# Dense attention stage: values become the stationary operand of the weighting, transposed probabilities stream in two float32r parts, and VectorE takes tile work up once per unit

## What is computed

```
q = axial(rms_norm(q, qn_b));  k = axial(rms_norm(k, kn_b))      # two rotations of 32 dims
s = einsum('bqhgd,bkhd->bhgqk', q, k) * 64 ** -0.5               # prompt: 512 keys, sample: 1024 keys
p = softmax(s, axis=-1)
o = einsum('bhgqk,bkhd->bqhgd', p, v)
```

## Time and profile before

| | |
|---|---|
| median of 3 runs | 3947.97 us (3947.69 to 3953.81) |
| profiled execution | 3949.25 us, span 3947.4 us |
| dense stage | 0 to about 673 us of the span |
| busy over the span | PE 96%, PEld 90%, DVE 67%, ACT 53%, POOL 22% |
| granted TensorE clock, mean | 0.986 |

### The profile page before, as it was taken

One profiled execution on the slowest core, in us unless ns is written; L12 is line 12 of the kernel. 1 busy time (PEld: TensorE's weight loads), 2 busy tenths in 40 slices (PEclk: granted clock), 3 DMA queues, 4 the chain that ended last, 5 costly groups with the idle time before them and its releaser, 6 DMA issues. The chain is left out here.

```text
span 3947.4 us, 70746 instructions
## 1 busy us (share of the span) xinstructions
PE 3802.8 (96%) x24950; PEld 3570.8 (90%) x24950; DVE 2643.0 (67%) x5354; ACT 2096.3 (53%) x3837; POOL 854.5 (22%) x1367
## 2 busy tenths in 40 slices
PE   8999999999999889999999999999997999999998
PEld 7989989999987789999999989999886999999998
DVE  6565664676665677777777757777536777777775
ACT  6544554555552255565556556555323556655654
POOL 5132230333330011121111133323000111111112
PEclk9999999999999999999999999999898999999999
DMA  3000001122124378887788731000335788778874
GB/s 110 10 22 7 24 17 36 45 69 64 49 97 154 130 248 248 264 256 241 243 266 255 242 91 47 31 24 16 137 139 192 234 251 271 246 238 252 270 245 134
DMA packets 492025, 583.96 MB, mean 148 GB/s; under 512 B 21536, under 2 KB 447520, under 8 KB 491808
## 3 DMA queue, kind: packets, MB, share of 16 engines
q1 hardware_dynamic: 473952, 522.44, 41.1%
q0 software_dynamic: 15680, 50.34, 5.4%
q10 hardware_dynamic: 2176, 8.39, 0.5%
HBM read 514.89 MB, written 66.22 MB: 147 GB/s over the span
## 5 line engine op out<-in xcount | busy, mean ns | idle before, releaser
L1774 DVE TENSOR_TENSOR wl<-raw,wh 128x2048 fp32r<-128x2048 f32 x384 | 876.1, 2289 | 193.6 <-ACT wh L1717 175.0
L1717 ACT CAST wh<-raw 128x2048 fp32r<-128x2048 f32 x384 | 730.5, 1910 | 24.4 <-DMA raw<-in_w_gate 22.1
L1890 PE MATMUL ps_g<-xT,wh 128*128 128x384 f32 x2048 | 594.2, 356 | 0.3 <-DVE xT L1780 0.3
L1890 PE MATMUL ps_u<-xT,wh 128*128 128x384 f32 x2048 | 593.5, 356 | 0.0
L1892 PE MATMUL ps_g<-xT,wl 128*128 128x192 f32 x2048 | 477.5, 254 | 0.0
L1892 PE MATMUL ps_u<-xT,wl 128*128 128x192 f32 x2048 | 477.3, 254 | 0.0
L151 PE MATMUL psP<-ring_high,hTh 128*128 128x384 f32 (+1 forms) x1344 | 459.8, 342 | 12.5 <-DVE ring_low L826 6.3
L153 PE MATMUL psP<-ring_high,hTl 128*128 128x384 f32 (+1 forms) x1344 | 441.3, 328 | 0.0
L152 PE MATMUL psP<-ring_low,hTh 128*128 128x384 f32 (+1 forms) x1344 | 440.9, 328 | 0.0
L1080 PEld LDWEIGHTS psO<-V,pT 128*128 128x128 f32 x3456 | 421.4, 194 | 20.3 <-issue 10.2
L1080 PE MATMUL psO<-V,pT 128*128 128x64 f32 x3456 | 419.5, 274 | 4.9 <-ACT pT L759 3.0
(11 more groups left out here) (219 smaller groups left out, 7715.4 us busy)
## 6 DMA issues: line engine op xcount, KB each, us to landing
raw<-in_w_gate SPq DMA_DIRECT2D x128, 1024.0 KB, 5.7
raw<-in_w_up SPq DMA_DIRECT2D x128, 1024.0 KB, 5.8
raw<-in_w_down SPq DMA_DIRECT2D x128, 1024.0 KB, 8.3
xb<-in_x SPq DMA_DIRECT2D x72, 256.0 KB, 2.8
out_y<-yb SPq DMA_DIRECT2D x24, 512.0 KB, 2.6
h_rows<-hb SPq DMA_DIRECT2D x24, 512.0 KB, 3.0
ring_raw<-in_w_a SPq DMA_DIRECT2D x24, 384.0 KB, 3.8
xb<-in_x SPq DMA_DIRECT2D x12, 512.0 KB, 4.6
```

The lines of the kernel that those rows point to most:

```text
L1717: act.copy(wh[:, j % SPL], raw[:, j % RAW]).then_inc(w_high, 1)
L1774: dve.tensor_tensor(wl[:, j % SPL], raw[:, j % RAW], wh[:, j % SPL].bitcast(F32), ALU.subtract)\
L1890: both = lambda **fl: pe.matmul(ps[:, f, 0:2 * CAP], wh[:, j % SPL, k, fs], xT[:, k].rearrange("p h c -> p (h c)"), **fl)
```

## The change

Only the dense stage changes.

- V u becomes two events, V u.0 and V u.1, a batch each. `V` now holds the values' high and low parts side by side (128 columns, float32r) and is the stationary operand; `pT` holds the high and low parts of a batch side by side, and 256 columns stream per block, one float32r matmul each. The result `psO` is [value part, query] and must be summed over the two streamed parts (`join`, DVE, into `oT`), transposed back (event O, PE, into a room of `psT`), summed over the two value parts (`add_halves`, DVE) and divided (`divide`, ACT).
- Each batch of probabilities is now copied by ACT (high part) and then subtracted by DVE (`turned_low`). `pT` has three slots.
- V u.1 stands behind R u+1; O u stands behind S u+3. So `psT` sees three fillings per unit where it saw two.
- The maximum is written negated straight to `nbias` (the factor 1/8 goes into the gains once), which saves one small DVE instruction per unit.
- DVE: the maximum of S u+2 is taken at V u.0, after the output work; and there one stage of the current tile follows (`tile_up_to(age + 1)`), where before all stages could follow in one unit. T p therefore comes when p is three units old, not one.
- ACT empties `psP` behind the copies of an R that follows, and makes `V` in two instructions (`v32`, `V`); POOL subtracts for the low part of `V`, and for the prompt tiles between units POOL also does the straight products of the rotation.
- The rotation table is loaded in four pieces without its repetitions; `xb` has three buffers, in the room of `qT`.

```diff
             elif kind == "U":
-                events.append(("R", n))
                 if n + 2 < len(self.units):
                     turn_up_to(self.units[n + 2][3])
                     events.append(("S", n + 2))
-                if turned + 1 in since and since[turned + 1] >= 1:
+                if turned + 1 in since and since[turned + 1] >= 3:
                     turn_up_to(turned + 1)
                 for p in since:
                     since[p] += 1
-                events.append(("V", n))
+                if n:
+                    events.append(("O", n - 1))
+                events.append(("V", n, 0))
...
+            if kind == "U" and n:
+                events += [("R", n), ("V", n - 1, 1)]
...
         for e in self.events:
-            if e[0] in "TN":
+            if e[0] in "TNO":
...
-                act.mul(V[:, t, :], psP[:, nh * HD:NC], rt[:, steps[s]["order"], t:t + 1]).then_inc(evacuated, 1)
+                if dense:
+                    if p >= 2:
+                        act.wait_ge(v_split, p - 1)
+                    act.mul(v32[:, b, :], psP[:, nh * HD:NC], rt[:, 0, t:t + 1])
+                act.mul(V[:, t, 0:nkv * HD], psP[:, nh * HD:NC], rt[:, steps[s]["order"], t:t + 1]).then_inc(evacuated, 1)
...
+            def divide(u):
+
+                segs = units[u][1]
+                act.wait_ge(rden_ready, u + 1)
+                act.wait_ge(o_added, u + 1)
+                for c, (h, t, *_) in enumerate(segs):
+                    out = osb[:, (units[u][0] * NT + t) % OR, h]
+                    ins = act.mul(out, out, rden[:, u % 4, c:c + 1])
+                ins.then_inc(o_done, 1)
...
+            def turned_low(u, k):
+                slot = work.spot(u, k)[0]
+                dve.wait_ge(pT_act, batch0[u] + k + 1)
+                dve.tensor_tensor(pT[:, slot, :, 1, :], room_of("R", u, k).rearrange("p (x c) -> p x c", c=P),
+                                  pT[:, slot, :, 0, :].bitcast(F32), ALU.subtract).then_inc(pT_dve, 1)
+
+            def join(u):
+
+                segs = units[u][1]
+                dve.wait_ge(pv_done, batch0[u] + 2)
...
+                for c in range(len(segs)):
+                    ins = dve.tensor_reduce(oT[:, u % 2, c * P:(c + 1) * P], o_half(u, c).rearrange("p (f c) -> p c f", f=2),
+                                            AX.X, ALU.add)
+                ins.then_inc(o_summed, 1)
...
-                if e[0] == "R":
+                if e[0] == "R" and dense:
+                    turned_low(e[1], 0)
+                    if e[1]:
+                        join(e[1] - 1)
+                    turned_low(e[1], 1)
...
-                if e[0] == "V":
+                if e[0] == "V" and dense:
+                    if e[2] == 0:
+                        maxima()
+                        tile_up_to(age + 1)
+                        age = min(age + 1, 2)
...
+            def weigh_batch(u, k):
+                segs = units[u][1]
+                if k == 0:
+                    both = u > 0 and max(len(segs), len(units[u - 1][1])) > 1
+                    if u - 1 + both > 0:
+                        pe.wait_ge(o_summed, u - 1 + both)
+                    pe.wait_ge(v_split, units[u][3] + 1)
+                copied(u, k)
+                slot = work.spot(u, k)[0]
+                for x, (c, j) in enumerate(units[u][2][k]):
+                    k0, nk = segs[c][2:4]
+                    ins = pe.matmul(o_half(u, c), V[:, k0 + j, :], pT[:, slot, x, :, :].rearrange("p f c -> p (f c)"),
+                                    start=(j == 0), stop=(j == nk - 1))
+                ins.then_inc(pv_done, 1)
+
+            def turn_output(u):
+                pe.wait_ge(o_summed, u + 1)
+                room_free(("O", u))
```

More of the change, by code:

```diff
@@ L371, in dense_order @@
                 events.append((kind, n))
-        return events
+        return events + [("V", len(self.units) - 1, 1), ("O", len(self.units) - 1)]
     def by_act(self, u, k):
-        return k == 0 or (self.dense and u % 2 == 1)
+        return k == 0
     def count_batches(self):
@@ L525, in weights, with between_units, x_half, o_half @@
         return steps[i // turns]["w"][i % turns].rearrange("p (q k c) -> q p k c", q=WQ, c=NC)[q % WQ]
+    def between_units(p):
+        return p >= NT and p % NT < PT
+    def x_half(x):
+        return x_places[x % XH][:, :] if dense else xb[:, x % XH]
+    def o_half(u, c):
+        return psO[:, c * 2 * P:c * 2 * P + 2 * P] if len(units[u][1]) > 1 else psO[:, u % 2 * 2 * P:u % 2 * 2 * P + 2 * P]
     def raw_quarter(q):
@@ L578, in load_constants @@
                     sp.dma_start(gains[:, s, :], st["gain"]).then_inc(const_in, 16)
-                sp.dma_start(rope[:, :, :, :, :], table).then_inc(const_in, 16)
+                if dense:
+                    for tiles, at, c in ((slice(0, NT), slice(0, NT), 0), (slice(0, 1), slice(NT, NT + 1), 2 * R1)):
+                        sp.dma_start(rope[:, at, 0:R1], table[:, 0, tiles, 0, c:c + R1]).then_inc(const_in, 16)
+                        sp.dma_start(rope[:, at, R1:3 * R1], table[:, 0, tiles, 1, c:c + 2 * R1]).then_inc(const_in, 16)
+                else:
+                    sp.dma_start(rope[:, :, :, :, :], table).then_inc(const_in, 16)
                 if masks is not None:
@@ L616, in _ @@
                         load_w(e[1] // NT * WQ + RING + 2 * e[2] + quarter)
-                if e[0] == "V":
+                if e[0] == ("O" if dense else "V"):
                     for p in tile_done(e[1]):
@@ L679, in _ @@
                         pool.wait_ge(const_in, 16 * NCONST)
+                        if dense:
+                            chain.link(pool.tensor_scalar(gains[:, 0, 0:nq * HD], gains[:, 0, 0:nq * HD], SCALE, None, ALU.mult))
                         first = False
@@ L788, in _ @@
                 if e[0] == "T":
+                    if dense:
+                        squares()
                     high(e[1])
@@ L791, in _ @@
                         exponentials_up_to(scored_units)
+                if e[0] == "O":
+                    divide(e[1])
                 if e[0] == "P":
[L793 removed]
+                    exponentials_up_to(scored_units)
                     squares()
[L795 removed]
+                    if e[2] == 1 and dense:
+                        to_evacuate.append(e[1])
+                    elif e[2] == 1:
                         evacuate(e[1])
@@ L916, in output @@
                 p = i * NT + t
-                if h == 0:
-                    for x in range(p, p + (ns if dense else 1)):
-                        if x >= OR:
-                            dve.wait_ge(stored[x % OR], 16 * (x // OR))
+                if p >= OR:
+                    dve.wait_ge(stored[p % OR], 16 * (p // OR))
                 dve.wait_ge(pv_done, batch0[groups[g][-1] + 1])
@@ L963, in _ @@
                     maximum(e[1])
-                    if dense:
-                        tile_up_to(2)
+                if e[0] == "O":
+                    if e[1] == UT - 1:
+                        join(e[1])
+                    add_halves(e[1])
                 if e[0] == "T":
@@ L974, in _ @@
                     tile_up_to(3)
-                    tile, stage = e[1], 0
+                    tile, stage, age = e[1], 0, 0
                     if not dense:
@@ L1084, in weigh @@
                     off += len(segs)
+            def weigh_batch(u, k):
[15 more added lines that the diff above has]
+                room_free(("O", u))
+                for c in range(len(units[u][1])):
+                    ins = pe.transpose(room_of("O", u)[:, c * P:(c + 1) * P], oT[:, u % 2, c * P:(c + 1) * P], ident)
+                ins.then_inc(o_turned, 1)
             idle_bank = psS[:, 0, 0:P]
```

159 lines of the change are left out of this document (117 added, 42 removed).

## The result

The changed kernel takes 3998.73 us (median of 4 runs, 3997.44 to 4000.5), the kernel before beside it 3947.83. The ratio is 1.0128, 95% interval 1.0116 to 1.0139: 51 us slower, where the prediction had 21. The direction is as forecast, the size is not. The profiled execution took 3999.81 us.

What follows compares the result with a forecast made beforehand. PE alone was taken to set the pace, with VectorE becoming as full after the change. Terms -47.0 - 1.0 + 26.9 + 18.8 + 12.6 + 3.0 + 7.3 = +20.6 on 3949.25 gave 3969 us; range 3928 to 4001.

Steps and rivals of the forecast that it cites:

- a turn with its scale done: Turning a tile between units: T, high part, low part and next R share psT's room, delaying R u+1 by 1.65 us.
- Stretches, start and tail: Edges of the dense stage: +3.0 us for three tile stretches, +3.0 for the first group's start, +1.3 for the last unit.
- PE's cover: Single units: VectorE's other work lay hidden under PE's 3.54 us before; in the fuller loop it comes out as added time.
- the likeliest case: Whole kernel: the forecast itself, 3969 us, with its own range 3956 to 3985; chance 0.45.
- S follows float32r now and loses its 0.1 of switching: 0.91: Step in PE's sum for a single unit: S takes 0.91 us, part of the 2.93 that replaces 3.54.
- rival 1: VectorE keeps slack: its unit is under about 2.85, the loop is PE's 2.95, -19 us, 3929; chance 0.24.
- The forced pair: Once per group two tiles are turned directly before an S needing both: unit 9.67 us, +18.8 us over four groups.
- twelve tiles between units: Stages and turning of four tiles in each of three groups: 12 x (1.2 + 1.65 - 0.61) = +26.9 us.
- the weights: W on ScalarE and VectorE before the next R's copy: +12.6 us for ten in units, +3.0 for those in projections.
- double units: Second join and longer addition make VectorE's unit 3.5 us: 24 x -0.04 = -1.0; eight W there add 9.6.
- 4: Rival: join is dear, 0.69 us at 512 elements' price, +0.27 in each of 120 units, +32, 4001 us; chance 0.15.

Runs made afterwards that it cites:

- With VectorE relieved: Changed kernel with the row maximum taken over the first half of the scores only, 0.54 us less VectorE per unit: 3983.85 us, ratio 1.0093.
- with the waits filled: Changed kernel with useless matmuls in PE's waits, seven ahead of each forced turn and six ahead of the S needing it: 3976.18 us, ratio 1.0075.
- A better order with fillers: Changed kernel with scaled tiles turned early, fourth tile projected earlier, weights before exponentials, fillers at forced turns, first two W behind the turn: 3960.80 us, ratio 1.0026.

## Why the prediction was right or wrong

**Right.** The single unit without tile work: 3.05. `psO` at 0.56 per batch, `join` 0.415, `add_halves` 0.27, `low` and `high` as read; a turn with its scale done, 1.86 where 1.65 was put. Stretches, start and tail together within 1.9 us. The direction: what comes out beside the units is more than the units win. The reason given for it, that VectorE's tile work loses PE's cover, carries only a part: the stages and the later turn cost 57 us where VectorE has room. The measured time lies in the wide range (3928 to 4001) and outside the likeliest case's (3956 to 3985).

**Right for another reason.** The prediction made PE's sum 2.93 and let VectorE's 3.00 and the join close the loop at 3.05. PE alone is 3.05: "S follows float32r now and loses its 0.1 of switching: 0.91" didn't come, S takes 0.98, and the last batch 0.59. With VectorE relieved the unit stayed. So rival 1's condition (VectorE under 2.85) doesn't bring its time: with 0.54 us taken from VectorE in every unit the kernel took 3983.85 us and not 3929.

**The step that failed: "The forced pair".** The chain was right in kind (T, high, low, scale, T, high, low, S), its length was not; 9.67 became 12.76, and 0.1 to 0.8 more in the next unit. From the start of the unit:

| | forecast | measured | with the waits filled |
|---|---|---|---|
| first T | 2.0 | 3.97 | 3.97 |
| second T | 5.45 | 6.80 | 6.80 |
| S | 7.9 | 9.64 | 9.28 |
| end of the unit | 9.67 | 12.76 | 10.98 |

The start of the chain was missed by 2.0 us: the room for the first T comes free only behind the second tile's rotation (0.9 us of VectorE) and a W (1.0), which I had counted in another term and not in the wait for the room. Putting that W behind the turn brought the first T forward by 0.9 to 1.1. From the first T to the second it is 2.83 where I had 3.45. The end was missed by the clock, which I had named as unpriced: 1.8 us in the unit and 0.8 in the next at the second pair, 1.4 to 1.8 and 0.2 to 0.8 at all four. The term is +37.8 as sorted by units, +30.9 on the forecast's own footing, instead of +18.8.

**Missed: three of the "twelve tiles between units" aren't spread.** Tiles 15, 27 and 39 are needed by an S one unit before the rule of three would turn them, so they are turned ahead of it, with the scale not done: 5.4 each instead of 2.2. The nine others cost 1.4: the stages 0.19 and 0.33 in their units instead of 1.2 in all, and the units around their projections gain 0.3 more than the plain ones. The sum of the term looks right (28.8 against 26.9) by luck.

**Missed: the weights.** The W do show in double units: the one behind unit 32 costs 1.4 in unit 33, which fell from 4.96 to 3.6 when it was moved, and the one behind unit 33 is part of the pair's late start. With them the double units are +3.3 on the forecast's footing, where -1.0 + 9.6 was put. Six inside projections cost 13.6, where +3.0 was put, since ScalarE now has an exponential ahead of them that waits for VectorE's late maximum, and behind two of the three waits of 2.7 us the clock is at half. Issuing the weights first took 7.4 us from the three projections.

**Missed: 8.3 us behind the dense stage.** The prediction had nothing there. They go with more half clock; why there is more of it is open.

**What the two halves are worth.** The gain of the streamed weighting is real, 0.49 us in a plain single unit, 47 if all 96 are put down with it. Against it stand 98 us. A better order with fillers took 38 of them, part of that behind the dense stage; some 60 remain that no order here removed, so that the best is 10 us behind the kernel before. Of the rivals, 4 came nearest in time (4001) and for a wrong cause: `join` is at its cheap price.

## What to carry to other kernels

When a faster engine leaves another as full as itself, price the exceptions first: list each place where the order forces a chain across engines directly ahead of its use, and see whether its early links (here the scale, and GpSimd's root behind it) were done a unit before. A part that is meant to make room, such as one stage per unit, can be dear alone: measure both parts apart, and expect them not to add. Waits of 2 us on TensorE, one behind the other, may cost their length and then the clock behind them; the granted clock of such windows comes before any explanation, and cheap matmuls in the waits are a test of it and here were a remedy. And where a stage that wasn't touched moves by 0.3%, one trace of each kernel doesn't tell whose doing it is.

## What the runs showed of the hardware that I had not expected

- In the kernel before, the clock was 1.00 in the whole dense stage. In the changed one it fell to its lower level (0.5 of 2.4 GHz, 1.2 GHz) at each of the four pairs, among waits of 2.5, 2.3 and 1.9 us that followed each other, and at each of the three single forced turns, with waits of 2.2 and 1.9; it was 0.51 over the 7 us from 275.90, and the `psS` matmuls started 0.42 to 0.56 apart instead of 0.23. With twenty useless matmuls in the waits of a pair it stayed at 1.00 at three of the four.
- A wait of 2.7 us by itself didn't settle the clock. The three projections with W have one each: in the changed kernel the clock was at half behind the second and third (11.2 and 11.1 us) and not behind the first (10.0); with the pairs' waits filled it was at half behind the first (10.8) and not behind the others (10.0 each). So such a wait alone doesn't decide it, and these traces don't show what does.
- 256 elements reduced to 128 out of PSUM took VectorE 0.415 us, and 256 reduced to 4 out of SBUF 0.413: no surcharge for a PSUM source shows.
- An engine that is full on the page need not set the pace: VectorE was busy for 45.3 of 45.9 us in the single units, and taking 0.54 us from VectorE in each left the unit at 3.05.
